# The delta-rule stages of a two-block model: chunk order, 64-column blocks and the place of the inverse

## What is computed

```python
def gated_delta_rule(q, k, v, g, beta):          # chunks of 64 tokens, 8 heads of 128
    gc = jnp.cumsum(to_chunks(g), axis=-1)
    decay = exp(gc_i - gc_j) on the lower triangle
    kb = kc * bc[..., None]
    a_mat = where(strict, einsum('nbhid,nbhjd->nbhij', kb, kc) * decay, 0.0)
    rhs = concatenate([vc * bc, kb * exp(gc)], axis=-1)
    value, kcd = triangular_solve(a_mat + eye, rhs)       # unit lower triangle
    attn = einsum('nbhid,nbhjd->nbhij', qc, kc) * decay
    def step(s_st, xs):                                   # over the four chunks
        v_new = val_i - kcd_i @ s_st
        o = q_inter_i @ s_st + attn_i @ v_new
        s_st = s_st * exp(gl_i) + kst_i^T @ v_new
```

## Time and profile before

| | us |
|---|---|
| median of 3 runs | 2710.01 (2709.78 to 2712.34) |
| the profiled execution | 2712.49 |
| its span, first to last instruction | 2710.7 |
| granted TensorE clock, mean | 0.958 of 2.4 GHz |

### The profile page before, as it was taken

The page is one execution under the profiler, slowest core; times in us unless marked ns, Lnnn a source line. Parts: engine busy times, 40 slices in busy tenths (PEclk is TensorE's granted clock), DMA queues, the critical chain, the costliest instruction groups (busy, mean ns, idle before and its releaser), DMA issues.

```text
span 2710.7 us, 40577 instructions
## 1 busy us (share of the span) xinstructions
PE 2572.4 (95%) x17728; PEld 2367.6 (87%) x17728; DVE 1601.6 (59%) x2170; ACT 1043.9 (39%) x1224; POOL 110.5 (4%) x142
## 2 busy tenths in 40 slices
PE   8999799999997999889989999999998998998998
PEld 8999479999996699789979989799998998997997
DVE  5555465564463654557856555755676555786555
ACT  4333343333333443245024334443465334501432
POOL 0001000000010000001000000100001000100000
PEclk9999599999997899989989999999999998998999
DMA  7568035555582165354015554465545654511553
GB/s 241 186 178 216 23 111 186 187 195 185 185 201 85 40 211 186 110 156 140 16 47 189 188 162 154 140 192 190 181 133 166 187 180 125 155 32 31 180 187 125
DMA packets 320800, 405.35 MB, mean 150 GB/s; under 512 B 48688, under 2 KB 281232, under 8 KB 320624
## 3 DMA queue, kind: packets, MB, share of 16 engines
q1 hardware_dynamic: 314960, 383.63, 45.6%
q0 software_dynamic: 5664, 19.13, 2.4%
HBM read 401.68 MB, written 1.05 MB: 149 GB/s over the span
## 4 chain that ended last, share of the span: by engine, by line
PE 86%; DVE 7%; ACT 2%; issue 2%; DMA 1%; POOL 1%; SPq 0%; DVEq 0%; POOLq 0%; ACTq 0%
PE ps L415 24%; PE ps L416 24%; PE ps L417 24%; PE ps L2227 1%; PE ps L2236 1%; PE ps L2235 1%; PE ps L1021 1%; DVE ws L1261 1%; ACT w_hi L402 1%; PE ps L681 1%; PE ps L2156 1%; DMA raw<-in_w_in 1%; DVE w_lo L409 1%; DVE ws L1249 0%; PE ps L2274 0%
## 5 line engine op out<-in xcount | busy, mean ns | idle before, releaser
L409 DVE TENSOR_TENSOR w_lo<-raw,w_hi 128x2048 fp32r<-128x2048 f32 (+1 forms) x363 | 813.5, 2266 | 182.2 <-ACT w_hi L402 182.0
L402 ACT CAST w_hi<-raw 128x2048 fp32r<-128x2048 f32 (+1 forms) x363 | 686.6, 1892 | 526.3 <-PE ps L417 426.8
L415 PE MATMUL ps<-aT_hi,w_hi 128*128 128x256 f32 x2816 | 805.2, 286 | 0.9 <-DVE w_lo L409 0.9
L416 PE MATMUL ps<-aT_lo,w_hi 128*128 128x256 f32 x2816 | 803.0, 285 | 0.0
L417 PE MATMUL ps<-aT_hi,w_lo 128*128 128x256 f32 x2816 | 802.7, 285 | 0.0
L415 PEld LDWEIGHTS ps<-aT_hi,w_hi 128*128 128x128 f32 x2816 | 547.4, 194 | 4.4 <-DVE w_lo L409 1.1
L416 PEld LDWEIGHTS ps<-aT_lo,w_hi 128*128 128x128 f32 x2816 | 547.0, 194 | 3.3
L417 PEld LDWEIGHTS ps<-aT_hi,w_lo 128*128 128x128 f32 x2816 | 546.6, 194 | 0.0
L415 PE MATMUL ps<-w_hi,h_hi 128*128 128x512 f32 x928 | 363.4, 392 | 5.5 <-DVE h_lo L1527 4.2
L416 PE MATMUL ps<-w_lo,h_hi 128*128 128x512 f32 x928 | 362.4, 391 | 0.0
L417 PE MATMUL ps<-w_hi,h_lo 128*128 128x512 f32 x928 | 361.1, 389 | 0.0
(11 more groups left out here) (361 smaller groups left out, 2327.8 us busy)
## 6 DMA issues: line engine op xcount, KB each, us to landing
raw<-in_mlp_w SPq DMA_DIRECT2D x128, 1024.0 KB, 5.7
raw<-in_ffn_wd SPq DMA_DIRECT2D x44, 1024.0 KB, 4.9
raw<-in_ffn_wg SPq DMA_DIRECT2D x43, 1024.0 KB, 5.3
raw<-in_ffn_wu SPq DMA_DIRECT2D x43, 1024.0 KB, 5.3
raw<-in_gdn_w_in SPq DMA_DIRECT2D x32, 1024.0 KB, 5.7
raw<-in_mlstm_w_in SPq DMA_DIRECT2D x12, 1024.0 KB, 5.3
raw<-in_diff_w_in SPq DMA_DIRECT2D x12, 1024.0 KB, 5.1
raw<-in_w_in SPq DMA_DIRECT2D x8, 1024.0 KB, 6.4
```

What stands on the lines that cost most here:

```text
L402: nc.scalar.copy(used_part(hi_slot(n), n), used_part(raw[:, n % RAW, :], n)).then_inc(hi_ready, 1)
L409: nc.vector.tensor_tensor(used_part(lo_slot(n), n), used_part(raw[:, n % RAW, :], n), used_part(hi_slot(n), n).bitcast(F32), ALU.subtract) ...
L415: nc.tensor.matmul(dst, l_hi, r_hi, start=start, stop=False)
L416: nc.tensor.matmul(dst, l_hi, r_lo, start=False, stop=False)
```

## The change

Only the two delta-rule stages change, on all engines.

- Chunk order z0 z1, gates, k, v, q, z2 z3 (`gdn_columns`); the stage opens with `open_stage`. SP's wait for the parameters in layer 0 moves behind chunk 4.
- Decays, A, attention and all matrices of the inverse are stored as 64-column blocks [128, tile, head, 64], and each matmul takes one 64x64 block (`blocks`; `token_products` for A and attention with all 128 rows).
- A is built from k alone, scaled by columns; beta comes onto rows by a product with `same_chunk`. Beta k is no longer turned. The first level needs no product of its own for T^T; the right side of level 0 is a transpose by blocks.
- One level of the inverse per chunk: in chunk u `before(u)` issues `both(u - 10)`, `middle(u)`, between the two halves of the chunk's product, `right(u - 9)`. Values, state reads, attention and the first state gain lie in chunks 15 and 16.
- POOL takes the gates' gain, the keys for the state and the decayed queries.
- States, reads and new values are made by halves of the heads, the state update is a scalar_tensor_tensor for each head, the output from the state is accumulated with that within the chunk (queries are decayed beforehand), and ACT squares and sums it by head.
- The output is multiplied by `w_out` one token tile after the other (`out_by_tiles`).

The core of the diff (DVE's order at the end; its functions do what their names say):

```diff
-def gates_second(wi, gates, n):
-    chunks = [column_pieces(wi, [(c, CW)]) for c in range(0, gates, CW)]
-    return chunks[:1] + [column_pieces(wi, [(gates, n)])] + chunks[1:]
+def gdn_columns(wi):
+    q, k, v, z = ([(1024 * a + CW * c, CW) for c in range(4)] for a in range(4))
+    order = z[:2] + [(GDN_QKV + GDN_Z, GDN_AB)] + k + v + q + z[2:]
...
+    def tokens_product(pe, n, bank, width=CW, between=None):
...
                 if i:
                     sp.wait_ge(out_set, group_count(i - 1, GROUPS[i - 1] - 1))
...
+        def gained(c):
+            pool.wait_ge(gd_z.sem, gd_z.count(j, c))
+            z = g_z[:, :, 2 * c:2 * c + 2, :]
+            nc.gpsimd.tensor_tensor(z, z, g_gain.unsqueeze(1).unsqueeze(1).to_broadcast([P, TT, 2, P]), ALU.mult).then_inc(gd_zg.sem, 1)
...
+        gained(0)
+        gained(1)
+        inverse_root(0)
+        for t in range(TT):
+            pool.wait_ge(gd_kbe.sem, gd_kbe.count(j, t))
+            pool.wait_ge(gd_rk.sem, gd_rk.count(j, 0))
+            nc.gpsimd.tensor_tensor(g_k[:, t, :, :], g_k[:, t, :, :], g_rkes[:, t, :].unsqueeze(2).to_broadcast([P, HN, P]),
+                                    ALU.mult).then_inc(gd_kst.sem, 1)
+        pool.wait_ge(gd_er.sem, gd_er.count(j, 3))
+        for c in range(4):
+            pool.wait_ge(gd_silu.sem, gd_silu.count(j, 8 + c))
+            f = slice(2 * c, 2 * c + 2)
+            nc.gpsimd.tensor_tensor(g_er[:, f, :], g_er[:, f, :], g_qT[:, f, :], ALU.mult).then_inc(gd_qe.sem, 1)
+        inverse_root(1)
+        gained(2)
+        gained(3)
+        for t in range(TT):
+            pool.wait_ge(out_ss, group_count(i, t))
+            nc.gpsimd.tensor_tensor(head_rs(i, t), head_ss(i, t), mhalf[:, 0:HN], ALU.pow).then_inc(pool_chain, 1)
+            pool_steps[0] += 1
+            pool.wait_ge(pool_chain, pool_steps[0])
+            pool.wait_ge(gd_rq.sem, gd_rq.count(j, 0))
+            nc.gpsimd.tensor_tensor(head_rs(i, t), head_rs(i, t), g_r[:, 0, t, :], ALU.mult).then_inc(out_rs, 1)
...
+        def blocks(bank, lhs, rhs):
+            for h in range(HN):
+                for r in CK:
+                    last = nc.tensor.matmul(ps[r, bank, CHUNK * h:CHUNK * h + CHUNK], lhs[r, h, :], rhs(r, h), start=True, stop=True)
+            return last
+        def token_products(bank, lhs, rhs, t):
+            for h in range(HN):
+                for q, r in enumerate(CK):
+                    s = slice(t * P + CHUNK * q, t * P + CHUNK * q + CHUNK)
+                    last = nc.tensor.matmul(ps[r, bank, CHUNK * h:CHUNK * h + CHUNK], lhs[:, h, s], rhs[:, h, s], start=True, stop=True)
+            return last
...
+        def right(v):
+            for t in range(TT):
+                if v == 1:
+                    done(gd_T0, t)
+                else:
+                    done(inv_t, TT * (v - 1) + t)
+                blocks(4 + t, g_A[:, t, :, :], lambda r, h: g_T[r, t, h, :]).then_inc(inv_y.sem, 1)
+        def both(v):
+            for t in range(TT):
+                done(inv_ys, TT * (v - 1) + t)
+                if v < LEVELS - 1:
+                    blocks(4 + t, g_TT[:, t, :, :], lambda r, h: g_Y[r, t, h, :])
+                blocks(6 + t, g_Y[:, t, :, :], lambda r, h: g_TT[r, t, h, :]).then_inc(inv_z.sem, 1)
...
+                done(gd_kbe, TT - 1)
+                done(gd_vc, 3)
+            for hh in range(2):
+                for q in range(4):
+                    for r in CK:
+                        last = nc.tensor.matmul(ps[r, 4 + hh, q * P:(q + 1) * P], g_TT[r, t, 4 * hh + q, :], g_v[r, t, 4 * hh + q, :],
+                                                start=True, stop=True)
+                last.then_inc(gd_val.sem, 1)
...
+        def state_gain(c, hh):
+            t, r = c // 2, CK[c % 2]
+            for h in range(4 * hh, 4 * hh + 4):
+                last = nc.tensor.matmul(ps[:, 4 + hh, h % 4 * P:(h % 4 + 1) * P], g_k[r, t, h, :], g_value[r, t, h, :], start=True, stop=True)
+            last.then_inc(gd_p2.sem, 1)
...
+        def state_reads(c):
+            t, r, s = c // 2, CK[c % 2], slice(CHUNK * c, CHUNK * c + CHUNK)
+            for hh in range(2):
+                done(gd_S, 2 * (c - 1) + hh)
+                for h in range(4 * hh, 4 * hh + 4):
+                    last = nc.tensor.matmul(ps[r, 2 + hh, h % 4 * P:(h % 4 + 1) * P], g_kcdT[:, t, h, r], g_S[:, c % 2, h, :],
...
+            for hh in range(2):
+                for h in range(4 * hh, 4 * hh + 4):
+                    nc.tensor.matmul(ps[r, 6 * t + hh, h % 4 * P:(h % 4 + 1) * P], g_er[:, h, s], g_S[:, c % 2, h, :],
+                                     start=(h == 4 * hh), stop=False)
+        def chunk_output(t, hh):
+            for h in range(4 * hh, 4 * hh + 4):
+                for q, r in enumerate(CK):
+                    last = nc.tensor.matmul(ps[r, 6 * t + hh, h % 4 * P:(h % 4 + 1) * P], g_dec[r, t, h, :], g_value[r, t, h, :],
+                                            start=(t == 0 and q == 0 and h == 4 * hh), stop=(h == 4 * hh + 3))
+            last.then_inc(gd_o.sem, 1)
+        def before(u):
+            if u == 4:
+                sums()
+            if u == 6:
+                k_turned(0)
+            if u == 7:
+                k_turned(1)
+                square_sums(0)
+                square_sums(1)
+            if u == 8:
+                for c in (2, 3):
+                    square_sums(c)
+                for c in (2, 3):
+                    k_turned(c)
+            if u == 9:
+                for t in range(TT):
+                    done(gd_R, t)
+                    if t == 0:
+                        done(gd_kc, 3)
+                    nc.tensor.matmul(ps[:, 6 + t, :], same_chunk, ws[9][:, 512 * t:512 * t + 512], start=True, stop=True).then_inc(gd_brow.sem, 1)
+            if u == 10:
+                for t in range(TT):
+                    done(inv_t, t)
+                    blocks(4 + t, g_TT[:, t, :, :], lambda r, h: id64[r, :]).then_inc(inv_y.sem, 1)
+            if 11 <= u <= 15:
+                both(u - 10)
+            if 9 <= u <= 12:
+                v_turned(u - 9)
+            if 13 <= u <= 16:
+                square_sums(u - 9)
+            if u == 16:
+                attention(0)
+                values_reads(1)
+        def middle(u):
+            if u == 8:
+                for t in range(TT):
+                    if t == 0:
+                        done(gd_kc, 1)
+                    token_products(4 + t, g_kT, g_kT, t).then_inc(gd_kk.sem, 1)
+            if 10 <= u <= 14:
+                right(u - 9)
+            if u == 15:
+                values_reads(0)
+            if u == 16:
+                done(gd_z, 2)
+                attention(1)
+                first_gain()
...
+        open_stage(pe, n0, edge)
+        tokens_product(pe, n0 + 2, 3, GDN_AB)
...
+        for u in range(3, 17):
+            before(u)
+            if u in (4, 5):
+                done(gd_z, u - 4)
+            if u >= 6:
+                done(gd_conv, u - 6)
+            bank = (u - 1) % 3
+            if u < 15:
+                features_product(pe, n0 + u, bank, between=lambda: middle(u))
             else:
-                tokens_product(pe, n0 + m, (m - 1) % 3)
-            if m == 3:
-                pe.wait_ge(gd_g.sem, gd_g.count(j, 0))
-                pe.wait_ge(gd_tb.sem, gd_tb.count(j, 0))
...
+        def rows(t, r):
+            if r % 2 == 0:
+                pe.wait_ge(aT_lo_set.sem, aT_lo_set.count(xpass, 2 * t + r // 2))
+            pe.wait_ge(lo_ready, n + r + 1)
+            hi, lo, s = by_rows(hi_slot(n + r)), by_rows(lo_slot(n + r)), slice(t * P, (t + 1) * P)
+            for half in range(2):
+                c = slice(512 * half, 512 * half + 512)
+                for k in range(2):
+                    last = product(pe, ps[:, 2 * t + half, :], aT_hi[:, 2 * r + k, s], aT_lo[:, 2 * r + k, s], hi[:, k, c], lo[:, k, c],
+                                   r == 0 and k == 0, r == 3 and k == 1)
+                if r == 3 and 2 * t + half < 3:
+                    last.then_inc(y_bank.sem, 1)
+            if t:
+                last.then_inc(weights_used, 1)
+        turned_over(0)
+        for r in range(3):
+            rows(0, r)
+        turned_over(1)
+        rows(0, 3)
+        for r in range(4):
+            rows(1, r)
...
+        for u in range(3, 17):
+            if u == 7:
+                square_sums_set(0)
+            if u == 8:
+                first_level()
+            if 10 <= u <= 14:
+                inverse_set(u - 9)
+            if 3 <= u <= 14:
+                convolved(u - 3, (u - 1) % 3)
+            if u == 3:
+                differences()
+            if u == 7:
+                key_factors()
+            if 8 <= u <= 11:
+                v_scaled(u - 8)
+            if u == 9:
+                keys_decayed(0)
+            if 9 <= u <= 13:
+                right_set(u - 8)
+            if u == 9:
+                keys_decayed(1)
+            if u == 14:
```

(28 more changed lines are left out.)

825 lines of the change are left out of this document (409 added, 416 removed).

## The result

The changed kernel takes 2601.46 us (median of 4 executions, 2598.24 to 2606.36) against 2711.03 us (2709.78 to 2712.34, four executions): a ratio of 0.9602, 95% interval 0.9584 to 0.962. The profiled execution took 2598.47 us, its span is 2596.0.

A forecast was written before the change was run, and what follows sets the result against it. TensorE work end to end plus a few named waits was taken as the bound. Twice -84.2 us for the stages and -29.5 for the opening gave -113.7, and 2712.5 - 113.7 - 2.5 = 2596 us; own range 2576 to 2612.

The forecast's parts named there:

- Opening: Start of both delta-rule stages: products on tile 0 between the two turns, -17.5 us in layer 0, -12 in layer 3.
- Inverse: Inverse in the delta-rule stages: 64x64 blocks run side by side, 0.93 us a group, 30 groups; -31.7 us a stage.
- The first rival: Block matmuls: the quadrants run in single file, +35 us a stage, 2663 us; chance 0.15.
- Fits under the chunks: Chunks from 10 on: PE stays the longest with 12.0 us a chunk, DVE has 9.3 to 9.8.
- the allowances: New waits in each delta-rule stage: +4.8 us (0.4, 0.9, 1.5, 2.0).
- One sign: Between chunk 16 and the states: no stretch without DMA would be seen.
- the second rival: Chunks 9 to 15: DVE becomes the bound, held up by GpSimd's multiplications, +9 us a stage, 2614 us; chance 0.16.
- GpSimd: Ten new multiplications on GpSimd: 0.7 to 1.3 us per 512, all hidden, +2 us for meetings with DVE's splits.
- States: State stretch: half heads and an earlier first state leave about 1 us of PE's waits for DVE, -5.2 us.
- Turn and row products: Output of each stage: earlier first row product -4.2 us, row products at full clock -2.8.
- Next norm: Norm behind each delta-rule stage: bank 2 ends only 1.3 us before bank 3, +1 us.
- the third rival: Chunks 8 to 16: small blocks don't keep PE's clock up, 1.2 GHz adds up to 214 us, 2810 us; chance 0.05.

The follow-up runs named there:

- e1: Changed kernel with ScalarE's and VectorE's last two weight splits of a delta-rule stage moved behind token tile 0's squares in the following norm: 2587.76 us.
- e3: Changed kernel with SyncE's wait for the layer norm back behind chunk 1 in layer 0: 2613.2 us.
- e4: Changed kernel with TensorE turning both token tiles before the first product, as before the change: 2620.86 us.
- e6: Changed kernel with each inverse group's eight matmuls of one row half before the eight of the other, instead of in turn: 2644.07 us.
- e7: Changed kernel with GpSimd's ten multiplications of a stage on VectorE instead: 2607.86 us.
- e5: Changed kernel with levels 1 to 5 of the inverse, values, state reads and first state gain after chunk 16: 2616.72 us.
- e2: Changed kernel with output weights used in the order of before, both token tiles turned first: 2598.59 us.
- e10: Kernel of e1 plus the gates' product of token tile 0 before tile 1's turn and the taps turned and copied earlier: 2585.06 us.
- e9: Kernel of e1 run again, unchanged: 2588.12 us.

## Why the prediction was right, and where not

**Opening: right.** Predicted -17.5 and -12, measured -19.9 and -11.6 (-17.0 with e1's opening, which has the same instructions). Products start at 1135.79, 5.7 us behind the last product ahead of the mixer; the 1146 named lay 8.5 behind that mark. Of tile 0's six microseconds 4.6 stand between the turns and 1.5 behind the second, as drawn. e3 and e4 show both mechanisms, and that neither alone brings the sum.

**Inverse: right, and by the right row.** The level on both sides takes 3.95 us for 128 records, the four groups of 0.93 and the drain at the end. L951 of the earlier trace rows was the pattern to go by. The record starts lie 6 to 7 ns apart in a pair and 0.052 to the next pair, 0.058 from pair to pair. The first rival is refuted: both row halves write into one bank, on different partitions, and run side by side. By the Trainium skill, TensorEngine Tiling (Array Packing), section Restrictions and Gotchas, different row tiles can't access one bank at the same time; for tiles on different partitions of the bank the trace says otherwise, and the measurement decides. e6 comes nearest to that rival, with 18.5 us a stage for the blocks instead of 28; it isn't quite single file, since neighbours at the seams of the halves still overlap.

**Fits under the chunks: right, the allowances were not needed.** A chunk with a level takes 12.4 us against 12.0 (chunks 11 and 12; 12.9 in 13 and 14, which hold the square sums of q), the difference being four changes of array form of 0.09. Of the 4.8 us of new waits a stage only the taps' 0.35 came. That is the term of the sum that was mis-sized, by 4.4 us a stage. It explains the two stages together (-80.5 against -72.2), not each: layer 0 gained 6.4 us more than the sum, layer 3 only 1.9. One sign didn't come: in chunk 16, ahead of the states, the DMA engines do stand still (0.00 from 1298 to 1305). That DVE never holds PE up shows in DVE's groups from chunk 9 to 16 (busy us, mean ns | idle before):

```profile
L410 DVE TENSOR_TENSOR w_lo<-raw,w_hi 128x2048 fp32r<-128x2048 f32 x7 | 16.0, 2281 | 0.0
L2626 DVE TENSOR_TENSOR ws<-ps,gb 128x512 f32<-128x512 f32 x10 | 6.9, 692 | 3.6 <-PE ps L2152 3.5
L2633 DVE TENSOR_TENSOR ws<-ws,ps 128x512 f32<-128x512 f32 x10 | 6.8, 683 | 1.5 <-PE ps L2152 1.5
L2632 DVE TENSOR_TENSOR ws<-ws,ps 128x512 f32<-128x512 f32 x8 | 5.5, 687 | 9.6 <-PE ps L2152 9.6
```

DVE waits for PE's blocks 14.6 us over these, PE for DVE never; the second rival is refuted, and e7 adds that even with GpSimd's work DVE isn't the bound. The other side of this term: e5 puts the worth of the cover at 4 us a stage. All but these 4 of the 40 us that the stretch lost go to less and cheaper work and fewer waits in the states.

**GpSimd: right on both ends.** 128x512 took 1.27 to 1.29 us, the upper end of 0.7 to 1.3. The meetings with DVE (+2 a stage) cost PE nothing. They are to be seen; GpSimd's timeline in the changed kernel:

```profile
1222.54 1.90 POOL L2125 TENSOR_TENSOR ws<-ws,small 128x1024 f32<-128x1024 f32 x1 [20.33 <-DVE ws L2639]
1225.60 3.88 POOL L2125 TENSOR_TENSOR ws<-ws,small 128x1024 f32<-128x1024 f32 x1 [1.16 <-DVE ws L2639]
```

and DVE's:

```profile
1221.25 1.22 DVE L2639 TENSOR_TENSOR ws<-ws,small 128x1024 f32<-128x1024 f32 x1
...
1223.94 1.58 DVE L2639 TENSOR_TENSOR ws<-ws,small 128x1024 f32<-128x1024 f32 x1
1225.44 2.28 DVE L410 TENSOR_TENSOR w_lo<-raw,w_hi 128x2048 fp32r<-128x2048 f32 x1
```

Where the two overlap, one of them stretches: DVE's multiplication by 0.36 us, GpSimd's by 1.98 under a split that keeps its 2.28. The Trainium skill's page SBUF — State Buffer, section Who interferes with whom, has this contention, and the trace agrees that it exists; here the split went first, so that the rival's 2.3 us a meeting fell on GpSimd, which nobody waited for.

**States: right.** One wait of 0.32 us is left where 1 was allowed; reads to last output take 19.3 us.

**Turn and row products: right in kind, 2 us too much in all.** 3.9 us to the first product, with two waits (0.81 and 2.01) where one of 3 to 4 was named; the products take 22.9 and 24.4 us with tile 1's turn instead of 21.7. In layer 0 no half clock stands in them. What was mis-sized is the matmul of 512 columns: the prediction had four times 0.054, 0.216 us, the trace has one every 0.227 at full clock, 21.8 us for 96 instead of 20.7. In layer 3 half clock comes on top (the stretch has 0.93).

**Next norm: wrong, by 14 us.** The step said that bank 2 ends only 1.3 us before bank 3, +1 a stage. It looked at when the banks are complete, and not at what stands on ACT and DVE ahead of the norm: two splits whose weight slots now come free only with token tile 1. The prediction had itself argued from ACT standing at a late chunk in the opening, and did not ask the same question at the other end of the stage. The term was +7.5 and +8.3 us; e1 takes 6.9 and 6.3 of it back, e2 shows that it cancels the whole gain of the order by tiles.

**Clock: the third rival is refuted, and so is an argument against it.** The granted clock is 1.00 from 1163 to 1324. But the prediction also held that in the kernel before the products behind the square sums of one column go on at full clock. They don't; the stretches behind the two runs of square sums in layer 0 are:

```profile
1228.50:1233.00 4.50, 4.50 (x26) 4.50 (x26) 4.43 (x8) 1.27 (x1) 0.00 (x0) 0.62 0.32 112
1250.00:1257.00 7.00, 7.00 (x37) 7.00 (x37) 3.65 (x5) 0.52 (x1) 0.00 (x0) 0.54 0.34 115
```

PE has no idle time there. The two runs of square sums take 3.6 and 4.6 us; in the changed kernel none is longer than 1.8 us, and the clock stays at 1.00. So narrow matmuls with half clock behind them were to be seen before the change. Of the half clock that the sum took back (4 a stage) more came: 1162.6 to 1393.8 has 0.94 before, 1151.7 to 1324 has 0.98 after.

So the forecast of 2596 us met the median of 2601 with two misses of opposite sign, +8 and -14, and with a median that can itself lie several us to either side (2598 and 2606 in executions of one kernel). The changed stages alone gave 108.0 us of the 113.7; the 7.4 us of the part ahead of them, which the change doesn't touch, covered that in the profiled execution. It was right on the mechanisms named, but for the next norm's, and lucky on the rest. Its own range, 2576 to 2612, said to be the sum without the allowances or with them doubled, doesn't follow from them either: 4.8 us a stage make it 2586 to 2606, which still holds the 2601.

## What to carry to other kernels

When a step moves where a buffer or weight slot comes free, list for every engine what is queued behind the transfer into it; work that is long ready behind a split that isn't is the first thing to reorder. Before giving a gain to overlap, price the same work uncovered: here the cheaper matmuls carried nearly all, and the cover 4 of 40 us. A small matmul that fills a quarter of the array cost half its time here when its neighbour took the other row half, so put the loop over the halves innermost; and compare marks within the trace, since the median also holds the clock of stretches that nobody changed.

## Of the hardware, not expected

- Two 64x64 f32 matmuls on different row halves, into different partitions of one PSUM bank, run side by side (32 records in 0.93 us; 0.058 us for each record where the halves don't alternate).
- While DVE's split of 128x2048 runs, GpSimd's multiplication of 128x1024 takes 3.88 us instead of 1.90, and the split its 2.28; in layer 3 the numbers are the same (3.88, 2.28).
- The granted clock falls to 1.2 GHz within the 6 us of the gates' 16-column matmuls (1151.5 to 1157.8; 1.00 up to 1155, 0.57 from 1155 to 1163), although PE has no idle time of over 0.4 us there, and in the kernel before it is at 0.62 and 0.54 behind 3.6 and 4.6 us of one-column square sums. In e10, with two runs of 3 us and no long wait, chunk 3 keeps 1.00.
- The same instructions in front of the first mixer take 1127 to 1139 us from one execution to the next, by how long the clock stays at the lower level in the attention of the first block (885 to 903: 0.60 in e1, 0.86 in e9).
